# Prompt attention of a hybrid decoder step: one merged square per head turned on TensorE, parted in two by VectorE

## What is computed

```python
dist = pos_q[:, :, None] - pos_k[:, None, :]
valid = (dist >= 0) & (dist < WINDOW) & (pos_k[:, None, :] >= 0)   # WINDOW = 128
...
s = einsum(q, k) * scale - slopes * dist
s = where(valid, s, -1e30)
m = maximum(max(s, axis=-1), sink)
p = exp(s - m)
den = sum(p, axis=-1) + exp(sink - m)
o = einsum(p / den, v)
```

## Time and profile before

| what | value |
|---|---|
| time, median of 3 runs | 1295.09 us (1295.01 to 1295.23) |
| span of the profiled execution, first to last instruction | 1292.5 us |
| TensorE busy | 1271.2 us, 98% |
| VectorE busy | 811.1 us, 63% |
| ScalarE busy | 578.6 us, 45% |
| GpSimd busy | 189.8 us, 15% |

### The profile page before, as it was taken

The page is one execution under the profiler, slowest core; times in us unless marked ns, Lnnn a source line. Parts: engine busy times, 40 slices in busy tenths (PEclk is TensorE's granted clock), DMA queues, the critical chain, the costliest instruction groups (busy, mean ns, idle before and its releaser), DMA issues. The chain is left out here.

```text
span 1292.5 us, 24746 instructions
## 1 busy us (share of the span) xinstructions
PE 1271.2 (98%) x10221; PEld 1244.3 (96%) x10221; DVE 811.1 (63%) x1220; ACT 578.6 (45%) x999; POOL 189.8 (15%) x182
## 2 busy tenths in 40 slices
PE   6999999999999999999999999999999999999997
PEld 5999999999998999999999999999999999999996
DVE  7701446654334655447888877677669885688874
ACT  5412333444434533336865555555463434234252
POOL 1000100000000122222353333232310000000021
PEclk9999999999999999999999999999999999999999
DMA  9998322222222543545336553544598666776533
GB/s 326 322 300 276 129 66 67 74 81 79 67 67 76 184 126 107 153 124 153 114 109 210 154 154 126 166 142 134 159 336 278 210 201 217 214 237 199 183 127 101
DMA packets 238556, 211.59 MB, mean 164 GB/s; under 512 B 17169, under 2 KB 219797, under 8 KB 233565
## 3 DMA queue, kind: packets, MB, share of 16 engines
q1 hardware_dynamic: 237580, 209.66, 51.3%
q10 hardware_dynamic: 865, 0.36, 0.1%
HBM read 161.97 MB, written 49.04 MB: 163 GB/s over the span
## 5 line engine op out<-in xcount | busy, mean ns | idle before, releaser
L597 PE MATMUL psum<-xh,b_lo 128*128 128x264 f32 x908 | 257.7, 284 | 0.0
L595 PE MATMUL psum<-xh,b_hi 128*128 128x264 f32 x908 | 256.8, 283 | 0.7 <-DVE b_lo L1840 0.7
L596 PE MATMUL psum<-xl,b_hi 128*128 128x264 f32 x908 | 256.2, 282 | 0.0
L595 PE MATMUL psum<-dh,e_hi 128*128 128x264 f32 x896 | 254.9, 285 | 0.0
L596 PE MATMUL psum<-dl,e_hi 128*128 128x264 f32 x896 | 253.9, 283 | 0.0
L597 PE MATMUL psum<-dh,e_lo 128*128 128x264 f32 x896 | 253.7, 283 | 0.0
L595 PE MATMUL psum<-h_hi,w_hi 128*128 128x384 f32 (+1 forms) x624 | 208.0, 333 | 2.8 <-issue 1.7
L596 PE MATMUL psum<-h_lo,w_hi 128*128 128x384 f32 (+1 forms) x624 | 201.5, 323 | 0.0
L597 PE MATMUL psum<-h_hi,w_lo 128*128 128x384 f32 (+1 forms) x624 | 201.3, 323 | 0.0
L595 PEld LDWEIGHTS psum<-xh,b_hi 128*128 128x128 f32 x908 | 170.4, 188 | 1.0 <-DVE b_lo L1840 0.9
L596 PEld LDWEIGHTS psum<-xl,b_hi 128*128 128x128 f32 x908 | 170.5, 188 | 0.0
(11 more groups left out here) (317 smaller groups left out, 2376.9 us busy)
## 6 DMA issues: line engine op xcount, KB each, us to landing
down_raw<-in_w_down_dram SPq DMA_DIRECT2D x72, 512.0 KB, 6.0
dr<-ff_scratch SPq DMA_DIRECT2D x28, 1056.0 KB, 8.0
up_raw<-in_w_up_dram SPq DMA_DIRECT2D x76, 256.0 KB, 3.7
ff_scratch<-st SPq DMA_DIRECT2D x64, 264.0 KB, 3.3
ada_p<-in_w_ada_dram SPq DMA_DIRECT2D x8, 2048.0 KB, 10.2
ff_scratch<-st SPq DMA_DIRECT2D x32, 396.0 KB, 3.6
w_raw<-in_w_in_dram SPq DMA_DIRECT2D x20, 512.0 KB, 4.8
gates_scratch<-g_out SPq DMA_DIRECT2D x16, 528.0 KB, 3.2
```

The lines of the kernel that those rows point to most:

```text
L595: mm(out, whi, rhi, start=first, stop=False)
L596: mm(out, whi, rlo, start=False, stop=False)
L597: return mm(out, wlo, rhi, start=False, stop=last)
```

## The change

The two halves of a head's scores are joined before the exponential. For i > 0 `soft_a` takes the larger of the two halves place by place into the first 128 columns of `pr` (the half that is not seen holds about -1e30), and everything after works on one square of 128 columns per head. `turn_probs` turns four squares instead of eight, all in bank 4 + 2*kv. The two ScalarE copies `pt_copy` are gone. In their place VectorE runs `part(i, kv)`: it multiplies the turned squares by a triangle of ones and zeros, `seen`, which GpSimd writes once at the start, and gets the own block's part of `pT`; then it subtracts this from the turned squares and gets the block before's part. In block 0 there is only the first of the two.

`part(i, 0)` stands on VectorE behind `qk_low(i + 1)`, `part(i, 1)` behind `split_lo(u + 2)`, and `pool_group(i + 1)` moves from in front of these to behind `d_lo`. In the last block `part(7, 1)` stands behind the first `a_lo`.

```diff
@@ turn_probs (TensorE)
-                for kk in ([1] if i == 0 else [0, 1]):
-                    bank = 3 + 2 * kv + kk
-                    wait(pe, free[bank], take(bank, ("pt", i, kv, kk)))
-                    for c in range(G):
-                        last = nc.tensor.transpose(psum[:, bank, c * P:(c + 1) * P], pr[:, kv, c, kk * P:(kk + 1) * P], ident[:, :])
-                    last.then_inc(ready[bank], 1)
+                bank = 4 + 2 * kv
+                wait(pe, free[bank], take(bank, ("pt", i, kv)))
+                for c in range(G):
+                    last = nc.tensor.transpose(psum[:, bank, c * P:(c + 1) * P], pr[:, kv, c, merged(i)], ident[:, :])
+                last.then_inc(ready[bank], 1)
@@ exps (ScalarE; the function pt_copy and its calls are taken out)
-                    fn(pr[:, kv, c, k0:256], pr[:, kv, c, k0:256], ACT.Exp, bias=nmx[:, kv, c:c + 1], accum_out=rsum[:, kv, c:c + 1])
+                    fn(pr[:, kv, c, merged(i)], pr[:, kv, c, merged(i)], ACT.Exp, bias=nmx[:, kv, c:c + 1], accum_out=rsum[:, kv, c:c + 1])
@@ soft_a, soft_b, part (VectorE)
-                ch.step(nc.vector.tensor_reduce(mx[:, kv, :], pr[:, kv, :, k0:256], AX.X, ALU.max))
+                if i:
+                    ch.step(tt(pr[:, kv, :, 0:P], pr[:, kv, :, 0:P], pr[:, kv, :, P:2 * P], ALU.max))
+                ch.step(nc.vector.tensor_reduce(mx[:, kv, :], pr[:, kv, :, merged(i)], AX.X, ALU.max))
...
-                tt(pr[:, kv, :, k0:256], pr[:, kv, :, k0:256], rden[:, kv, :].unsqueeze(2).to_broadcast([P, G, 256 - k0]), ALU.mult).then_inc(p_done, 1)
+                tt(pr[:, kv, :, merged(i)], pr[:, kv, :, merged(i)], rden[:, kv, :].unsqueeze(2).to_broadcast([P, G, P]), ALU.mult).then_inc(p_done, 1)
+            def part(i, kv):
+                done = there(("pt", i, kv))
+                bank, _ = turn["pt", i, kv]
+                own, before = (pT[:, kv, kk, :].rearrange("p (c q) -> p c q", c=G) for kk in (1, 0))
+                turned = psum[:, bank, :].rearrange("p (c q) -> p c q", c=G)
+                if i == 0:
+                    dve.wait_ge(const_done, 5)
+                else:
+                    there(("o", i - 1))
+                last = tt(own, turned, seen[:, :].unsqueeze(1).to_broadcast([P, G, P]), ALU.mult)
+                if i:
+                    ch.step(last)
+                    last = tt(before, turned, own, ALU.subtract)
+                last.then_inc(done, 1)
@@ VectorE's loop over the blocks
-                if i < 3:
-                    pool_group(i + 1)
+                part(i, 0)
                 split_lo(u + 2)
+                if i + 1 < BLK:
+                    part(i, 1)
                 if i < 4:
                     dve.wait_ge(d_hi_done, i + 1)
                     tt(d_lo[:, :], z[:, U0 + i, :], f(d_hi[:, :]), ALU.subtract).then_inc(d_lo_done, 1)
+                if i < 3:
+                    pool_group(i + 1)
@@ the loop over S_ORDER behind it
                 tt(lo, src, f(hi), ALU.subtract).then_inc(s_lo_done, 1)
+                if n == 0:
+                    part(BLK - 1, 1)
@@ start (GpSimd)
+            nc.gpsimd.affine_select(out=seen[:, :], in_=ones[:, :], compare_op=ALU.is_ge, fill=0.0, base=0, pattern=[[1, P]],
+                                    channel_multiplier=-1).then_inc(const_done, 1)
```

More of the change, by code:

```diff
@@ L225, with merged @@
 S_ORDER = (0, 1, 2, 4, 5, 6, 3, 7)
+def merged(i):
+    return slice(P, 2 * P) if i == 0 else slice(0, P)
 def landed(u):
@@ L1264, in _ @@
             branch_hi(0)
-            pt_copy(BLK - 1, 1)
             branch_hi(1)
```

15 lines of the change are left out of this document (2 added, 13 removed).

## The result

| what | before | changed |
|---|---|---|
| time, median of 4 runs | 1295.05 us (1294.13 to 1295.23) | 1286.95 us (1286.79 to 1287.11) |
| ratio of the times | | 0.9942 (0.9929 to 0.9955) |
| span of the profiled execution | 1292.5 us | 1285.4 us |
| time of the profiled execution | not told | 1287.11 us |

The change gains 8.1 us of the median and 7.1 us of the span, the time from first to last instruction of one profiled execution. The prediction said 1288.9 and a range from 1288.2 to 1290.4: right in the direction, but the gain is 2 us larger, and the time lies under the range.

What follows compares the result with a forecast made beforehand. TensorE was taken to bound the kernel, busy for 98% of the span: 1292.5 less 6.2 us for the transposes, nothing returned, gives a span of 1286.3, plus 2.6 to the median, 1288.9 us; range 1288.2 to 1290.4.

Steps and rivals of the forecast that it cites:

- The transposes: Turns of blocks 1 to 7: 56 transposes go, 14 turns at 0.44 us, 6.2 us off TensorE's sequence.
- VectorE's new work: Maxima and parts on VectorE, 0.69 us per operation: about 15 us more in all, with no wait for TensorE.
- (b): The weighing in blocks 1 to 6, which waits for VectorE's `part(i, 1)`: 2.7 us spare.
- (c): Pooling group behind the parts, longest in block 2: just fits before the next scores' reader, 0.4 us to spare.
- (d): Last block, the tight place: `part(7, 1)` follows the first `a_lo` and ends before the weighing, 0.6 us spare.
- What ScalarE loses: 30 copies of 0.6 us each go and 56 exponentials halve: no cost, and no gain beyond the transposes.
- nothing returned: Whole program: TensorE's 6.2 us saving reaches the end undiminished, span 1292.5 to 1286.3 us; chance of this sum 0.85.
- Rival 3: Behind 432 us the gain is given back, for instance by the queue of weight loads: 1293 to 1295 us; chance 0.03.
- 2.6 us between span and median: Whole kernel: difference added to the forecast span of 1286.3 us to get the forecast median of 1288.9.
- Rival 4: Slower: the weighing waits for VectorE in every block; the gain becomes a loss at parts of 5.0 us; chance 0.02.

## Why the prediction was off

**The transposes: right.** 14 turns at 0.44 were 6.2 us; the starts give 6.06 over the 14 turns, and turning them twice gives 5.8 by the starts and 6.2 by the medians. Within the 6.06 two small errors nearly cancel: blocks 1 to 4 give 0.50 instead of 0.44 at their second turn, because the hold of 0.07 us by ScalarE's pooling copies goes too, and the first turn of block 7 gives only 0.05. There TensorE and then ScalarE read, in the changed kernel:

```profile
401.69 0.60 PE L810 MATMUL psum<-ident,pr 128*128 128x128 f32 x4
402.44 0.41 PE L601 MATMUL psum<-h_hi,w_hi 128*128 128x384 f32 x1 [0.15 <-ACT g_out L1202]
```

```profile
401.88 0.41 ACT L1202 ACTIVATE g_out<-psum 128x288 f32<-128x288 f32 x1 [2.70 <-PE psum L603]
```

The last gate unit goes by eighths over all three banks, so it can only begin once ScalarE has emptied the bank that was filled just ahead of the turn. The turn of eight hid this copy, the turn of four doesn't: 0.75 us from start to start where block 1 has 0.35. The prediction said of block 7 only what VectorE does.

**VectorE's new work: right.** 0.69 us for each kind; the sum of 15 us. The slack of each place came out nearly as worked out. (b) In block 1 the part had to end by 236.62, and no weighing waits. (c) In block 2 the pooling group ends, with the copy behind it, in front of the scores' reader with 0.3 us to spare (0.4 forecast):

```profile
272.70 0.41 DVE L1727 COPY pool_tail<-pool_s 128x480 f32<-128x480 f32 x1
273.44 1.29 DVE L1674 SCALAR_TENSOR_TENSOR pr<-psum,bias_p 128x512 f32<-128x512 f32 x2 [0.32 <-PE psum L800]
```

(d) In the last block, on VectorE and TensorE, the part is done at 408.25 and the weighing begins at 408.85, 0.6 us spare as forecast (for the earlier trace rows):

```profile
405.67 1.26 DVE L1737 TENSOR_TENSOR a_lo<-z,a_hi 128x1056 fp32r<-128x1056 f32 x1 [0.80 <-PE psum L603]
406.85 0.68 DVE L1700 TENSOR_TENSOR pT<-psum,seen 128x512 f32<-128x512 f32 x1
407.56 0.69 DVE L1703 TENSOR_TENSOR pT<-psum,pT 128x512 f32<-128x512 f32 x1
```

```profile
405.40 0.60 PE L810 MATMUL psum<-ident,pr 128*128 128x128 f32 x4
...
408.85 1.94 PE L821 MATMUL psum<-pT,v_tok 128*64 128x512 f32 x8
```

**"What ScalarE loses": the sum right, its reason wrong.** "No gain beyond the transposes, since TensorE hardly waits for it" reads "no wait in the list" as slack. At the pooling copies in blocks 1 to 4 there was none, so that without ScalarE's relief 2.0 us of the gain would have gone back. The change did both at once, so the total didn't show the error; I had asked of VectorE alone what is late next when TensorE comes earlier, and at both places where something was, here and in block 7's first turn, it is ScalarE.

**The sum, "nothing returned": the step that failed.** It took everything behind 432 us as a block that moves whole. It doesn't. The wait of 0.7 us at 763 us stood in the trace of before, outside the stretch that I had asked for TensorE's waits, and with it 0.98 us went. (The list counts idle time from the end of the matmul before; from start to start such a step is some 0.27 us longer.) Rival 3 looked there for a loss only, and at the DMA queues that the program writes, not at the fetch of code. That the number of TensorE's instructions ahead can decide it is shown in both directions: 34 more remove the wait from the kernel before, 64 or 70 more bring it into the changed one. It doesn't decide alone: the kernel that turns twice has as many as the kernel before and no wait. What removed it in the changed kernel therefore stays open between the missing transposes, which suffice in the kernel with half of the turns, and the edits on ScalarE and VectorE, which suffice in the one that turns twice. That it is the 16 KB piece which holds up the share is read from the records (one share of sixteen late, and the 150 units above), and no run takes the piece away by itself.

**The base: 0.8 us too high.** I set "2.6 us between span and median" as a constant. In every run since, time less span is 1.7 to 1.9 us, and runs of the kernel before with a span of 1292.5 took 1294.3. The profiled execution was then a quick one of some 1294.3 us, and the other 0.8 is spread between runs. From 1294.3 the same sum gives 1288.1. That the three runs on record lay within 0.22 us was luck: later ones of the same kernel spread over 4 us.

**Rival 4: its mechanism right, its threshold not.** "Some 0.9 more" is 6.2 us over seven blocks and forgets the last block's slack of 0.6, with which the gain is gone at parts of 4.7 us by the prediction's own figures, not 5.0. And the price of a late part was over twice what was worked out, because the second part also waits for the first, and the clock falls.

Together: 6.06 in the stretch, 0.98 at 763 us and 0.1 at the start make the 7.1 us between the spans, and the other 1.0 is the spread of the kernel before. Against the larger sets of runs of the kernel before (medians 1294.49 to 1294.76) the change gains 7.5 to 7.8 us, not 8.1. The range was too narrow because it held only what I could see in the stretch: its lower end allowed 0.7 us for all else.

**Open:** how the runs of the kernel before come to lie between 1293.4 and 1297.5; what in the changed kernel keeps the wait at 763 us away; why a piece 3.4 to 4.4 us after the request delays the first tile at some units and not at others, as at +3.56 in the kernel before and in the one that turns twice; and why added transposes move the piece by other amounts than I had worked out.

## What to carry to other kernels

Before pricing a saving on the engine that bounds, list all its waits in the whole program, also those far behind the edit: each of them can go or grow when instruction counts change, and a range for a small gain should hold the largest of them. Ask of every engine that shares a buffer with the bounding one, also of one that is only relieved, what its slack is against the saving itself; a removed cost and a relieved neighbour may be worth more together than apart (here 6.1 us against 4.1 and 0.25). A short list of waits doesn't tell that slack: compare the distance from start to start at a place with the same distance where nothing is waited for. Set the base by the time of the profiled execution, and where only its span is known, leave the difference to the median as a range.

## What the runs showed of the hardware

The fetch of an engine's own code is traffic like any other, and can be late for data. TensorE's pieces have 16 KB, one about every 15.3 us in the feed-forward part, and take 0.9 to 1.9 us each. Where one started 1.3 to 3.3 us after the request of a unit's first weight tile, the tile's last share of 16 landed at 5.0 to 5.9 us, against a median of 4.0 in units with no piece near, and where TensorE had little slack this cost 0.3 to 1.2 us per unit boundary, at one boundary or at three. In one comparison 4.4 us, 0.3% of this kernel, hung on nine transposes some 700 us earlier. The Trainium skill, "Runtime: NRT & Kernel Launch", section "Instruction fetch mechanics", says that each sequencer fetches 16 KiB blocks of 256 instructions through a queue of its own and that this is mostly hidden. For TensorE the trace agrees with the size; the pieces on the queue that ScalarE's and VectorE's added instructions moved have 8 KB here. What is late in these traces is the transfer beside it.

In a kernel that keeps its granted clock at 1.00 without them, single waits of 1.0 to 1.5 us on TensorE in each of blocks 1 to 4 left it there. Behind the second of two waits of 2.4 us, 32 us apart, it fell to the 1.2 GHz level for 3.4 us, and in a wait of 5.8 us for 6.8. This added some 4.5 us to the 15 us of waiting.
